# Other orders of work inside the two FFNs of a two-layer streaming encoder

## The reference

```python
def swiglu(h, w_gate, w_up, w_down):
    return (jax.nn.silu(h @ w_gate) * (h @ w_up)) @ w_down
...
        h = rms_norm(x, pre_ffn_g[l])
        x = x + rms_norm(swiglu(h, w_ffn_gate[l], w_ffn_up[l], w_ffn_down[l]), post_ffn_g[l])
```

## Time and profile before

| | |
|---|---|
| median of 3 runs | 1517.25 us (1509.87 to 1521.98) |
| profiled execution | 1516.38 us, span 1514.6 us |
| PE busy | 1401.6 us (93%) |
| DVE, ACT, POOL busy | 817.2, 525.9, 393.7 us |
| mean granted clock of TensorE | 0.970 |
| chain that ended last | PE 76%, DVE 14%, ACT 4% of the span |

### The profile page before, as it was taken

One profiled execution on the slowest core, in us unless ns is written; L12 is line 12 of the kernel. 1 busy time (PEld: TensorE's weight loads), 2 busy tenths in 40 slices (PEclk: granted clock), 3 DMA queues, 4 the chain that ended last, 5 costly groups with the idle time before them and its releaser, 6 DMA issues.

```text
span 1514.6 us, 20964 instructions
## 1 busy us (share of the span) xinstructions
PE 1401.6 (93%) x9193; PEld 1328.5 (88%) x9193; DVE 817.2 (54%) x909; ACT 525.9 (35%) x724; POOL 393.7 (26%) x306
## 2 busy tenths in 40 slices
PE   5999989899999999988998899898969999999976
PEld 4998979899999989977997689897959898988976
DVE  3347476765656546475435324357656565654625
ACT  4223252442525234343333121334324252523433
POOL 2052051533333314041002100014153333331405
PEclk9999999999999999989999899999989999999988
DMA  6221222122222212411143301213212222221231
GB/s 204 84 91 52 68 87 95 56 84 84 84 84 84 84 56 84 147 56 56 59 137 104 120 29 42 84 57 117 65 55 84 84 84 84 84 84 56 84 112 70
DMA packets 91857, 126.26 MB, mean 83 GB/s; under 512 B 2599, under 2 KB 76147, under 8 KB 91254
## 3 DMA queue, kind: packets, MB, share of 16 engines
q1 hardware_dynamic: 87688, 107.59, 21.7%
q0 software_dynamic: 3664, 16.80, 3.1%
q10 hardware_dynamic: 414, 0.54, 0.1%
HBM read 111.80 MB, written 13.12 MB: 82 GB/s over the span
## 4 chain that ended last, share of the span: by engine, by line
PE 76%; DVE 14%; ACT 4%; POOL 2%; issue 2%; DMA 2%; SPq 0%; DVEq 0%; ACTq 0%; POOLq 0%
PE ps L517 23%; PE ps L508 17%; PE ps L553 6%; PE ps L748 5%; PE ps L598 5%; PE ps L1004 4%; PE ps L763 4%; PE ps L707 3%; DVE wl L1053 1%; DVE wl L1188 1%; PE ps L650 1%; PE ps L977 1%; DVE xl L1092 1%; PE ps L990 1%; DVE up L1254 1%
## 5 line engine op out<-in xcount | busy, mean ns | idle before, releaser
L1053 DVE TENSOR_TENSOR wl<-stage,wh 128x2048 fp32r<-128x2048 f32 x57 | 140.1, 2458 | 93.6 <-ACT wh L1646 49.1
L1646 ACT ACTIVATE wh<-stage 128x2048 fp32r<-128x2048 f32 x47 | 89.7, 1908 | 198.5 <-PE ps L508 127.5
L2083 POOL TENSOR_TENSOR wsum<-stage 128x512 f32<-128x512 f32 x36 | 46.6, 1293 | 420.8 <-DVE wl L1188 257.9
L508 PE MATMUL ps<-xh,wh 128*128 128x320 f32 x448 | 103.1, 311 | 3.9 <-DVE qk L1059 2.4
L508 PE MATMUL ps<-xh,wl 128*128 128x320 f32 x448 | 102.7, 311 | 0.0
L508 PE MATMUL ps<-xl,wh 128*128 128x320 f32 x448 | 102.7, 311 | 0.0
L1188 DVE TENSOR_TENSOR wl<-wsum,wh 128x2048 fp32r<-128x2048 f32 x36 | 82.5, 2291 | 30.9 <-ACT wh L1675 30.7
L1724 ACT ACTIVATE gate<-ps 128x320 f32<-128x320 f32 x72 | 31.3, 434 | 162.6 <-PE ps L517 162.6
L1181 DVE TENSOR_TENSOR wbl<-stage,wbh 128x1024 fp32r<-128x1024 f32 x36 | 46.2, 1284 | 68.7 <-ACT wbh L1665 68.7
L508 PEld LDWEIGHTS ps<-xh,wh 128*128 128x128 f32 x448 | 75.3, 189 | 5.5 <-issue 2.9
L508 PEld LDWEIGHTS ps<-xh,wl 128*128 128x128 f32 x448 | 75.5, 189 | 0.0
(11 more groups left out here) (351 smaller groups left out, 4409.9 us busy)
## 6 DMA issues: line engine op xcount, KB each, us to landing
stage<-w_ffn_gate SPq DMA_DIRECT2D x22, 1024.0 KB, 5.3
stage<-w_ffn_up SPq DMA_DIRECT2D x22, 1024.0 KB, 5.3
stage<-w_ffn_down SPq DMA_DIRECT2D x22, 1024.0 KB, 5.1
stage<-w_in_odd SPq DMA_DIRECT2D x12, 1024.0 KB, 5.3
stage<-w_in_even SPq DMA_DIRECT2D x6, 1024.0 KB, 4.9
x_spill<-x POOLq DMA_DIRECT2D x2, 2560.0 KB, 8.2
x<-x_spill SPq DMA_DIRECT2D x2, 2560.0 KB, 10.1
stage<-w_out_even SPq DMA_DIRECT2D x4, 1024.0 KB, 5.1
```

The costliest lines, as they stand in the source:

```text
L508: last = pe.matmul(out[:, m, h, :], w[:, k, m * P:(m + 1) * P], mv_[:, k, h * HALF:(h + 1) * HALF], start=(k == 0 and n == 0), stop=(k == ...
L1053: dve.tensor_tensor(wl[:, s].rearrange("p k c -> p (k c)"), stage[:, s, :], f32(wh[:, s].rearrange("p k c -> p (k c)")), ALU.subtract).the ...
L1646: act.activation(wsh[:, u % 2, :], flat_stage(u), ACT.Copy).then_inc(w_hi, 1)
L2083: pool.tensor_tensor(s3, a11, a21, ALU.subtract).then_inc(s_sums, 1)
```

## The change

- A second table, `BEFORE`, says which pairs' gate and up stand ahead of each w_down: (0,1) (2,3) (4,5) (6,7) (8,9) (10). `PARTS` still says which pairs each w_down takes. So gate and up of 9 stand ahead of w_down of 8. Slots of hid go by `SLOT`, and w_down finds its tiles by `hid_tile`. Loads, group and unit numbers follow.
- Frame blocks, both layers: GpSimd makes the sums of pair 2's gate after the first two differences. B21 is split ahead of T3. In layer 0 the sums' low half goes ahead of the third y copy. In layer 1 odd tiles 0 and 1 go ahead of T4, tile 2 ahead of the sums, tiles 3 and 4 behind.
- w_down of 8 in layer 1: the sums' low half goes ahead of the even tiles.
- x is turned inside the third slab of the last part instead of the first.

```diff
+BEFORE = ((0, 1), (2, 3), (4, 5), (6, 7), (8, 9), (10,))
+SLOT = (0, 1, 0, 1, 0, 1, 0, 1, 0, 1, 0)
...
+        def hid_tile(n, k):
+            return 2 * SLOT[PARTS[n][k // 2]] + k % 2
...  # SP, load_ffn
-                    for p in part:
+                    for p in BEFORE[n]:
...  # PE, ffn and last_ffn
-                    for p in part_:
+                    for p in BEFORE[n]:
                         if p:
                             gate_up(0, p)
+                    place = lambda k: hid_tile(n, k)
...
-mv_[:, k, h * HALF:(h + 1) * HALF]
+mv_[:, place(k), h * HALF:(h + 1) * HALF]
...  # PE, turn_x
                         pe.wait_ge(x_back, 16 * 2)
+                        pe.wait_ge(y_tile_out, TT * (SLABS - 2))
...  # PE, last part
-                        even(units[0], 2 * n, views(units[0], nk, width, 0), nk, UW, ready, g, turning=True)
+                        even(units[0], 2 * n, views(units[0], nk, width, 0), place, nk, UW, ready, g)
+                        odd(units[0], 2 * n + 1, views(units[0], nk, width, UW), place, nk, UW)
+                        even(units[1], 2 * n + 2, views(units[1], nk, width, 0), place, nk, UW, turning=True)
                         pe.wait_ge(xF_done, TT)
-                        odd(units[0], 2 * n + 1, views(units[0], nk, width, UW), nk, UW)
-                        even(units[1], 2 * n + 2, views(units[1], nk, width, 0), nk, UW)
-                        odd(units[1], 2 * n + 3, views(units[1], nk, width, UW), nk, UW)
+                        odd(units[1], 2 * n + 3, views(units[1], nk, width, UW), place, nk, UW)
...  # DVE, ffn of layer 0, frame blocks
                         frames_lo(0, 3, B22, x[:, 4:8, 0:HALF])
+                        frames_lo(0, 4, B21, x[:, 4:8, HALF:])
                         y_out(ends[0], g, 0, False)
-                        frames_lo(0, 4, T3, x[:, 0:4, 0:HALF])
+                        frames_lo(0, 5, T3, x[:, 0:4, 0:HALF])
                         y_out(ends[1], g + 1, 2, False)
-                        frames_lo(0, 5, B21, x[:, 4:8, HALF:])
                         frames_lo(0, 6, T2, x[:, 4:8, 0:HALF])
                         frames_lo(0, 7, T4, x[:, 4:8, HALF:])
                         raw_lo(u, i)
+                        sums_lo(u)
                         y_out(ends[2], g + 2, 4, False)
-                        sums_lo(u)
                         y_out(ends[3], g + 3, 6, False)
...  # DVE, last_ffn, frame blocks
-                        frames_lo(1, 4, T3, x[:, 0:4, 0:HALF])
+                        frames_lo(1, 4, B21, x[:, 4:8, HALF:])
+                        frames_lo(1, 5, T3, x[:, 0:4, 0:HALF])
                         even_tiles(ends[0], left, False)
-                        frames_lo(1, 5, B21, x[:, 4:8, HALF:])
                         frames_lo(1, 6, T2, x[:, 4:8, 0:HALF])
+                        odd_tiles(ends[1], n, right, False, (0, 1))
                         frames_lo(1, 7, T4, x[:, 4:8, HALF:])
                         raw_lo(u, i)
+                        odd_tiles(ends[1], n, right, False, (2,))
                         sums_lo(u)
-                        odd_tiles(ends[1], n, right, False)
+                        odd_tiles(ends[1], n, right, False, (3, 4))
...  # DVE, last_ffn, w_down of 8
                         raw_lo(u, i)
+                        sums_lo(u)
                         even_tiles(ends[0], left, True)
-                        sums_lo(u)
                         odd_tiles(ends[1], n, right, True)
...  # ACT, last_ffn
-                for t in range(TT):
-                    act.wait_ge(xF_full, t + 1)
-                    act.activation(xF[:, t, :], span(tile_bank(1, 0), D), ACT.Copy).then_inc(xF_done, 1)
                 for m in range(4):
+                    for t in range(TT if m == 2 else 0):
+                        act.wait_ge(xF_full, t + 1)
+                        act.activation(xF[:, t, :], span(tile_bank(1, 0), D), ACT.Copy).then_inc(xF_done, 1)
...  # POOL, frames_sums
                 pool.tensor_tensor(b12, b22, b12, ALU.subtract).then_inc(t_sums, 1)
+                weight_sums(layer, PLAIN, 0)
                 pool.wait_ge(t_sums, 4 * layer + 1)
...
-                pool.wait_ge(b_ready, 7 * layer + 5)
+                pool.wait_ge(b_ready, 7 * layer + 4)
                 pool.tensor_tensor(b21, b21, b22, ALU.subtract).then_inc(t_sums, 1)
```

More of the change, by code:

```diff
@@ L78, in pair_group @@
 def pair_group(layer, p):
-    before = sum(p > part[-1] for part in PARTS) * 4 if layer == 0 else 0
+    before = sum(p > pairs[-1] for pairs in BEFORE) * 4 if layer == 0 else 0
     return (G_FF0, G_FF1)[layer] + 2 * p + before
 def down_group(n):
-    return pair_group(0, PARTS[n][-1]) + 2
+    return pair_group(0, BEFORE[n][-1]) + 2
 CORE = (("streams", 0), ("streams", 1), ("chunk", 0), ("chunk", 1), ("streams", 2), ("streams", 3),
@@ L495, in _, with unit @@
         def _(pe):
[L496 removed]
+            def unit(u, g, mh, ml, nk=KB, ready=None, wv=None, place=None):
                 pe.wait_ge(w_lo, u + 1)
@@ L507, in unit @@
                             for h in range(2):
-                                last = pe.matmul(out[:, m, h, :], w[:, k, m * P:(m + 1) * P], mv_[:, k, h * HALF:(h + 1) * HALF],
+                                last = pe.matmul(out[:, m, h, :], w[:, k, m * P:(m + 1) * P], mv_[:, place(k) if place else k, h * HALF:(h + 1) * HALF],
                                                  start=(k == 0 and n == 0), stop=(k == nk - 1 and n == 2))
@@ L591, in spread_half, with part @@
                           start=True, stop=True).then_inc(r_full, 1)
-            def part(wv, out, mh, ml, m, h, ks, nk):
+            def part(wv, out, mh, ml, m, h, ks, nk, place=None):
                 vh, vl = wv
@@ L607, in last_y_unit @@
                 for m, h in ((0, 0), (1, 0), (0, 1)):
-                    part(wv, out, mh, ml, m, h, range(nk), nk).then_inc(y_blocks_full, 1)
+                    part(wv, out, mh, ml, m, h, range(nk), nk, place).then_inc(y_blocks_full, 1)
                 pe.wait_ge(acc_empty, g)
@@ L612, in last_y_unit @@
                 now = min(nk - 1, 6)
-                last = part(wv, out, mh, ml, 1, 1, range(now), nk)
+                last = part(wv, out, mh, ml, 1, 1, range(now), nk, place)
                 if now == nk:
@@ L617, in last_y_unit @@
                 if now < nk:
-                    part(wv, out, mh, ml, 1, 1, range(now, nk), nk).then_inc(w_used, 1)
+                    part(wv, out, mh, ml, 1, 1, range(now, nk), nk, place).then_inc(w_used, 1)
             def boundary(B, u, blocks=2):
@@ L694, in ffn @@
                         for j in range(4):
-                            unit(u, g + j, hh, hl, nk=nk, wv=views(u, nk, width, j * UW))
+                            unit(u, g + j, hh, hl, nk=nk, wv=views(u, nk, width, j * UW), place=place)
                         continue
@@ L732, in turn_x, with even @@
                     last.then_inc(xF_full, 1)
-                def even(u, slab, wv, nk, width, ready=None, g=None, turning=False):
+                def even(u, slab, wv, place, nk, width, ready=None, g=None, turning=False):
                     pe.wait_ge(w_lo, u + 1)
@@ L752, in even, with odd @@
                     last.then_inc(w_used, 1)
-                def odd(u, slab, wv, nk, width):
+                def odd(u, slab, wv, place, nk, width):
                     pe.wait_ge(w_lo, u + 1)
@@ L762, in odd @@
                             for j, (w, mv_) in enumerate(((wv[0], hh), (wv[1], hh), (wv[0], hl))):
-                                last = pe.matmul(ps[:, tile_bank(1, t), 0:width], mv_[:, k, tile(t)], w[:, k, :],
+                                last = pe.matmul(ps[:, tile_bank(1, t), 0:width], mv_[:, place(k), tile(t)], w[:, k, :],
                                                  start=(k == 0 and j == 0), stop=(k == nk - 1 and j == 2))
@@ L1323, in even_tiles, with odd_tiles @@
                     y_tile(t, cols, add, tile_bank(0, t))
-            def odd_tiles(end, n, cols, add):
-                for t in range(TT):
+            def odd_tiles(end, n, cols, add, tiles=range(TT)):
+                for t in tiles:
                     if t < TT - 1:
```

76 lines of the change are left out of this document (39 added, 37 removed).

## The result

The changed kernel takes 1475.01 us, median of 4 runs (1473.08 to 1476.32), against 1515.45 for the kernel before (4 runs, 1509.87 to 1521.98): a ratio of 0.9731, 95% interval 0.9688 to 0.9773. Forecast were 1474.0, and 1465 to 1489 as the range. The profiled execution took 1473.08 with a span of 1471.3, 43.3 less than the span before.

The account below looks back on a forecast made before the run. TensorE, busy nearly the whole span, was taken to bound the kernel, with FFN waits of 36.3 us. Gains of 5.8 + 12.4 + 6.5 + 7.0 + 11.4 = 43.1 us off 1516.38 gave 1473.3, plus 0.87: 1474, range 1465 to 1489.

Parts of the forecast that it names:

- Frame blocks, layer 0: After pair 1: gate of pair 2 starts 4.1 us earlier, its 120 matmuls take 1.7 less; 5.8 us, bounds 3.8 to 7.8.
- a waiting operation before a newcomer: Frame blocks: VectorE and GpSimd operations with both inputs in SBUF exclude each other; first started goes first, then the waiting one.
- The row of 272.55: Layer 0 frame blocks before: VectorE's subtraction, 1.49 us alone, took 3.14, read as ending when GpSimd's 2.96 had passed.
- I take VectorE first: At 261.50, pair 1's product goes before GpSimd's fourth sum; otherwise 1.3 us per layer, 2.6 in all, is lost.
- Frame blocks, layer 1: After pair 1: gate of pair 2 starts at 1117.2 instead of 1129.6; 12.4 us, bounds 9.5 to 14.4.
- Gate of 9 ahead of w_down of 8: Pair 8, both layers: w_down finds hid finished, removing waits and slower matmuls; 6.5 us in layer 0, 7.0 in layer 1.
- Rival 2: Pair 8: the "issue" wait is not hid's or gate 9's weights come late; 13.5 shrinks to about 2, 1486; chance 0.08.
- x turned later: Tail: third slab ends 12.1 us earlier, less delay of its squares by the last turn's copy; 11.4 us, bounds 8.4 to 12.5.
- Rival 3: Tail: copies of turned x and squares hold each other up, each turn waiting 1.1; 5.5 us off, 1479; chance 0.10.
- Rivals 1 and 4: Number 4: TensorE's granted clock does not hold from 290 to 640; decides from 43 us lost time; slower; chance 0.03.
- Rival 1: Frame blocks fill up again through VectorE's collisions with GpSimd: 5.8 gone plus 8.9 in layer 1, 1489; chance 0.13.
- a long gap costs twice: TensorE in the FFNs: a long wait also lowers the granted clock of the matmuls behind it; a short one costs once.

Follow-up runs that it names:

- e5: The changed kernel with one wait added: GpSimd's fourth weight sum for pair 2's gate waits for VectorE's product of pair 1; 1473.77 us, ratio 0.9713.
- e1: The kernel before with only pair 9 ahead of w_down of 8, and layer 1's sums' low half ahead of the even tiles there; 1502.75 us, ratio 0.9901.
- e2: The kernel before with only the turning of x moved into the third slab of the last part; 1510.75 us, ratio 0.9946.
- e4: The changed kernel with GpSimd making the sums of pair 2's gate behind its fourth subtraction again; 1481.0 us, ratio 0.976.
- e3: The kernel before with only the new frame-block orders in both layers, GpSimd's early sums included; 1500.74 us, ratio 0.9883.
- e9: The kernel before with only GpSimd's sums for pair 2's gate moved ahead of its last two subtractions; 1510.39 us, ratio 0.9953.
- e10: e5 plus layer 0's raw low halves ahead of T4's and layer 1's third odd tile copy behind the sums' low half; 1473.96 us, ratio 0.9706.

## Why the prediction was right

**Frame blocks, layer 0: 5.2 of 5.8.** The schedule came out instruction by instruction, up to 1.1 late. VectorE in the changed kernel:

```profile
272.78 1.49 DVE L1206 TENSOR_TENSOR xb0l<-x,xb0h 128x1280 fp32r<-128x1280 f32 x1
...
275.59 2.81 DVE L1206 TENSOR_TENSOR xb3l<-x,xb3h 128x1280 fp32r<-128x1280 f32 x1
...
279.73 2.86 DVE L1206 TENSOR_TENSOR xq<-x,xq 128x1280 fp32r<-128x1280 f32 x1
283.98 1.49 DVE L1206 TENSOR_TENSOR xq<-x,xq 128x1280 fp32r<-128x1280 f32 x1 [1.40 <-ACT xq L1765]
...
287.13 2.28 DVE L1199 TENSOR_TENSOR wl<-wsum,wh 128x2048 fp32r<-128x2048 f32 x1
289.33 2.88 DVE L1111 COPY y<-ps 128x1280 f32<-128x1280 f32 x2
```

Forecast, shifted by the 0.52 us by which up of pair 1 ended later, were starts of 271.7 for B21's low half (272.78), 283.3 for T4's (283.98) and 286.7 for the sums' (287.13). The two collisions put in by the rule "a waiting operation before a newcomer" are there, 2.81 and 2.86 for 1.49. (The row of 272.55 was read loosely: its 3.14 us end at 275.69, not with GpSimd's subtraction at 274.34 but some 1.4 behind it. The later operation waits and then does its own work, and the schedule was worked out that way.) The lag is the product's 1.1 us at first, and 0.4 at the end, the steps between being a little shorter than reckoned. It also made the first y copy late: 1.0 us of TensorE's time where the forecast had 0.1 (0.2 in e5), hidden by the wait at the end. The gate started 0.4 later than forecast after up of pair 1 (30.49 against 30.1), and the 0.24 of the first matmul is the rest: the forecast let 19.27 become 17.6, and with a wait left it is 17.85.

**The step that failed: "I take VectorE first".** It was called a toss-up, 43.1 or 40.5 us, with the two within a tenth of a microsecond. GpSimd was first in both layers, and 41.1 was measured. e5 shows the price: 2.2, against 2.6. With it the stages would gain 43.3. The Trainium skill, page "SBUF — State Buffer", section "Who interferes with whom", has this meeting as an exclusive lock that goes by the order of issue. The changed kernel agrees in both orders: VectorE's product takes 2.59 us for 1.49 when GpSimd is 0.05 ahead, and GpSimd's third subtraction takes 4.04 for 2.96 when VectorE's low half of B21 started 0.23 ahead of it, at 272.78:

```profile
273.01 4.04 POOL L2086 TENSOR_TENSOR x<-x 128x1280 f32<-128x1280 f32 x1 [9.73 <-DVE xb1l L1206]
```

The page also exempts an operation of VectorE with at most one input in SBUF, outside its 2-port modes; the changed kernel agrees, where the product's forerunner, which reads PSUM, took 1.49 at 260.44 with GpSimd's sums running beside it.

**Frame blocks, layer 1: 11.5 of 12.4.** The same 1.1 on the product, of which 0.7 is left at the gate (29.95 us after up of pair 1, 29.3 forecast), and 0.24 for the first matmul behind a wait of 1.1, at a clock of 1.00. The order of odd and even tiles worked as worked out; GpSimd got no third subtraction in ahead.

**Gate of 9 ahead of w_down of 8: 13.1 of 13.5.** 14.08 for the 96 matmuls after, as in the other pairs, and 0.6 us of wait for an odd tile in layer 1 where 0.3 was forecast. Rival 2 is out: e1 removes the wait put to "issue" by the order alone. That it was hid's fits the kernel before: the low half of hid of pair 8 ends at 557.44, 0.2 ahead of TensorE's start at 557.65:

```profile
555.95 1.49 DVE L1207 TENSOR_TENSOR hl<-up,hh 128x1280 fp32r<-128x1280 f32 x1 [1.33 <-ACT hh L1746]
```

**x turned later: 11.3 of 11.4.** No wait for x is left in e2 or in the changed kernel. Rival 3 is out too; the last turn's wait is 1.1, and the closing chain starts 30.46 us after up of 10, where the forecast's slab (26.2) and squares (4.1) made 30.3. The two terms missed in opposite ways: the slab took 25.7, because the fifth turn stands behind its last matmul, and the chain started 4.8 after it.

**Rivals 1 and 4.** Rival 1 put 14.7 us on collisions that fill the frame blocks again; e4, with three more in each layer, lost 6.1. The clock held (1.00 for 340 us).

**What was right by luck.** The sum came out 2 us too high, and 2.2 us of the span's difference came from stretches that the change doesn't touch. The forecast also started from a median of 1517.25, and the four runs before now give 1515.45, 1.8 less. And layer 0's 6.5 at pair 8 was read off the very trace that it was measured against: the same stretch in the old order takes 93.7 to 93.8 us in e2, e3 and e9, against 94.88, and by those the gain is 5.2 to 5.3. 1474 against 1475 is closer than the method: its sum is good to 5%, single stages to 11%.

## What to carry to other kernels

Once one engine is busy for 93% of the span, list its waits, take each as a stretch between two fixed instructions, and write out the queue of the engine that it waits for, with every meeting of VectorE and GpSimd that both read SBUF twice; that gave five stages to within 1 us. Moving work of GpSimd out of such a stretch is worth what it takes from VectorE beside it, not only its own time. And judge an edit of 2 or 3 us by its stage in the trace, since whole times here move by more from one execution to the next.

## What the runs showed of the hardware

**Equal waits left different clocks.** e3's part at pair 8 of layer 1 is that of the kernel before: TensorE waits 3.5 us for hid and 1.9 for y in both. Windows over the two stretches that follow the first wait (columns as in the earlier trace rows), in the kernel before:

```profile
1388.59:1397.30 8.71, 8.71 (x31) 7.04 (x32) 1.65 (x2) 1.69 (x2) 0.00 (x0) 0.80 0.00 0
1397.30:1406.27 8.97, 7.08 (x32) 5.54 (x32) 7.76 (x10) 0.00 (x0) 3.53 (x3) 1.00 0.27 78
```

The same two in e3:

```profile
1373.00:1381.70 8.70, 8.70 (x31) 7.03 (x32) 1.65 (x2) 1.69 (x2) 0.00 (x0) 0.80 0.00 0
1381.70:1392.25 10.55, 8.66 (x32) 6.68 (x32) 7.76 (x10) 0.00 (x0) 5.03 (x4) 0.84 0.31 99
```

The second stretch takes 1.6 us more in e3, at 0.84 instead of 1.00. That is nearly all that e3's span lacks: it is 14.8 shorter than the span before, where the stages gain 16.6.

e2's shortfall is of the same kind. Its span is 4.3 us shorter than the span before, where its tail gains 11.3, so 7 us were lost ahead of the tail. 4.3 of them lie between layer 0's last w_down unit and layer 1's mixer (the chain's pieces of 7.32 and 4.46 us mark the two ends): 116.70 us, and 112.26 to 112.60 in the kernels before, after, e1, e3 and e4, with the same list of waits. Two windows of that stretch in the kernel before:

```profile
687.66:699.66 12.00, 9.59 (x64) 8.76 (x63) 8.07 (x8) 4.42 (x3) 1.18 (x1) 1.00 0.05 7
...
722.66:751.06 28.40, 28.40 (x194) 28.40 (x195) 10.79 (x5) 7.89 (x4) 0.00 (x0) 1.00 0.18 57
```

And in e2, at equal distances from the stretch's start:

```profile
689.38:701.38 12.00, 11.22 (x64) 10.60 (x64) 6.60 (x7) 1.91 (x1) 1.56 (x2) 0.86 0.00 0
...
724.38:752.78 28.40, 26.79 (x166) 25.97 (x167) 13.52 (x10) 7.88 (x4) 0.00 (x0) 0.94 0.24 74
```

The clock is 0.86 and 0.94 where the kernel before has 1.00. Of the other 2.7 us, 2.3 lie ahead of the end of up of pair 1 in layer 0 (262.17 against 259.89), in code that is the same; the rest is the balance of smaller differences. Five executions of e10 ran from 1467.36 to 1476.40, so the spread is no property of e2. What picks the clock behind a wait stays open here.

The 3.6 us wait at pair 8 of layer 0 shows it too: the 96 matmuls behind it took 16.95 in the kernel before, and 15.84, 15.74 and 15.85 in e3, e2 and e9. Windows over them, in the kernel before and in e3:

```profile
557.65:574.60 16.95, 16.95 (x98) 16.95 (x99) 8.31 (x6) 1.62 (x2) 3.17 (x3) 0.83 0.12 34
...
554.16:570.00 15.84, 15.84 (x98) 15.84 (x99) 8.31 (x6) 1.62 (x2) 3.18 (x3) 0.89 0.13 39
```

**A longer wait was not the dearer one.** Ahead of pair 2's gate in layer 0 TensorE waited 6.1 us in the kernel before and in e1, and the 120 matmuls behind it took 19.27 and 19.88 (granted clock 0.92 and 0.89); in e9 it waited 3.7 and they took 20.26 (0.87); in e4, 4.6 and 19.39 (0.91). Behind e4's 3.1 in layer 1 and behind waits of 0.5 to 1.1 us they took 17.85 (1.00), behind none 17.61. So "a long gap costs twice" holds for these waits of 3.6 us and more: with the 0.24 of a first matmul taken off, the second price lies between 1.4 and 2.6, and it doesn't go by the gap's length.
